# Sliding-window attention in a streaming encoder: rotary halves by a vector shuffle, weights scaled by a diagonal while they are turned, the sink as a column

## The reference

```python
q, k, v = split(x @ w_qkv)             # 16, 4 and 4 heads of 64
q, k = rope(q, pos), rope(k, pos)      # [x1*cos - x2*sin, x2*cos + x1*sin], halves of 32
s = einsum(q, k) * 64 ** -0.5          # prompt: own chunk of 64 and the two before it
m = max(max(s), sink)                  # sample: 128 cached keys and 32 new ones
p = exp(s - m)
p = p / (sum(p) + exp(sink - m))       # one sink logit for each head
o = einsum(p, v) @ w_out
x = x + o
```

## Time and profile before

| | |
|---|---|
| median of 3 runs | 1101.56 us (1100.84 to 1101.99) |
| the profiled execution | 1102.73 us |
| its span, first to last instruction | 1100.9 us |
| PE, DVE, ACT, POOL busy | 99%, 63%, 47%, 10% of the span |
| stage 8 and 9 on PE | from 781.4 to 880.2 us |

### The profile page before, as it was taken

How to read it: one execution, slowest core, us unless ns; L and a number is a source line. 1 busy time by engine, 2 the same in 40 slices (tenths; PEclk the granted TensorE clock), 3 DMA queues, 4 the chain that set the end, 5 groups by cost and what they waited for, 6 DMA issues and landing times.

```text
span 1100.9 us, 21167 instructions
## 1 busy us (share of the span) xinstructions
PE 1086.6 (99%) x8084; PEld 1070.0 (97%) x8084; DVE 696.9 (63%) x1082; ACT 516.8 (47%) x788; POOL 110.7 (10%) x142
## 2 busy tenths in 40 slices
PE   9999999999989999999999999999999999999998
PEld 8999999999989999999999999999988899999998
DVE  6766665567556766665547666645599766666442
ACT  6544443356663544444335444433466554444432
POOL 0000001100004300000110000011232510000011
PEclk9999999999999999999999999999999999999999
DMA  7544454434432644544434444544332244445431
GB/s 267 184 160 152 171 191 164 157 119 156 156 129 82 210 165 162 180 182 162 167 139 153 167 176 152 198 157 149 133 128 90 99 169 156 173 167 181 168 148 43
DMA packets 24596, 172.45 MB, mean 157 GB/s; under 512 B 3316, under 2 KB 3608, under 8 KB 5992
## 3 DMA queue, kind: packets, MB, share of 16 engines
q1 hardware_dynamic: 22520, 168.12, 42.7%
q0 software_dynamic: 960, 2.23, 0.6%
q10 hardware_dynamic: 1072, 1.51, 0.4%
HBM read 169.28 MB, written 2.57 MB: 156 GB/s over the span
## 4 chain that ended last, share of the span: by engine, by line
PE 92%; DVE 3%; ACT 3%; DMA 1%; issue 1%; POOL 0%; SPq 0%; DVEq 0%; ACTq 0%
PE acc L415 30%; PE acc L417 29%; PE acc L416 29%; DMA raw<-in_w 1%; PE num L480 1%; ACT whi L373 1%; DVE wlo L402 1%; PE acc L722 0%; PE num L675 0%; PE mb L694 0%; ACT L920 0%; DVE work L1221 0%; ACT work L986 0%; PE num L615 0%; ACT work L923 0%
## 5 line engine op out<-in xcount | busy, mean ns | idle before, releaser
L373 ACT ACTIVATE whi<-raw 128x1024 fp32r<-128x1024 f32 (+1 forms) x290 | 326.7, 1128 | 382.3 <-PE acc L417 360.4
L415 PE MATMUL acc<-xhi,whi 128*128 128x288 f32 x1680 | 501.2, 298 | 0.3 <-DVE wlo L402 0.3
L416 PE MATMUL acc<-xlo,whi 128*128 128x288 f32 x1680 | 495.6, 295 | 0.0
L417 PE MATMUL acc<-xhi,wlo 128*128 128x288 f32 x1680 | 494.0, 294 | 0.0
L402 DVE TENSOR_TENSOR wlo<-raw,whi 128x1024 fp32r<-128x1024 f32 (+1 forms) x290 | 385.0, 1328 | 164.5 <-ACT whi L373 154.1
L417 PEld LDWEIGHTS acc<-xhi,wlo 128*128 128x128 f32 x1680 | 316.4, 188 | 0.0
L415 PEld LDWEIGHTS acc<-xhi,whi 128*128 128x128 f32 x1680 | 314.9, 187 | 1.3 <-DVE wlo L402 0.6
L416 PEld LDWEIGHTS acc<-xlo,whi 128*128 128x128 f32 x1680 | 315.5, 188 | 0.6
L415 PE MATMUL acc<-ahi,whi 128*128 128x288 f32 x832 | 247.9, 298 | 0.9 <-DVE alo L1323 0.7
L416 PE MATMUL acc<-alo,whi 128*128 128x288 f32 x832 | 245.9, 296 | 0.0
L417 PE MATMUL acc<-ahi,wlo 128*128 128x288 f32 x832 | 245.1, 295 | 0.0
(11 more groups left out here) (215 smaller groups left out, 608.4 us busy)
## 6 DMA issues: line engine op xcount, KB each, us to landing
raw<-in_w SPq DMA_DIRECT2D x113, 1024.0 KB, 4.8
raw<-in_w SPq DMA_DIRECT2D x32, 1408.0 KB, 5.8
x<-in_xT SPq DMA_DIRECT2D x4, 288.0 KB, 5.3
raw<-in_w SPq DMA_DIRECT2D x4, 256.0 KB, 4.9
work<-bounce SPq DMA_DIRECT2D x1, 640.0 KB, 3.6
work<-in_cst POOLq DMA_DIRECT2D x1, 560.0 KB, 4.1
work<-in_c ACTq DMA_DIRECT2D x1, 514.0 KB
out_cp<-work POOLq DMA_DIRECT2D x4, 128.5 KB, 2.4
```

What stands on the lines that cost most here:

```text
L373: act.activation(dst, src, ACT.Copy).then_inc(hi_done, 1)
L415: pe.matmul(out, wh, hi[:, k, :], start=(first and n == 0), stop=False)
L416: pe.matmul(out, wh, lo[:, k, :], start=False, stop=False)
L417: mm = pe.matmul(out, wl, hi[:, k, :], start=False, stop=(last and n == len(tiles) - 1))
```

## The change

1. The swap leaves PE. The 64 dimensions of a head are reordered (in the weights, the tables and the cached keys) so that the two halves of a rotary pair are 16 partitions apart within a group of 32; DVE exchanges them with a shuffle straight from PSUM, and multiplies PSUM by the cosine. POOL multiplies the shuffled copy by the sine and adds. The copy, the PE matmul and the second PSUM bank for it are gone; the stage has 14 groups instead of 24.
2. The weights are no longer divided on DVE. They are turned by a float32 product with a diagonal matrix that holds the reciprocal sums, in place of a transposition with the identity. POOL makes the diagonals (identity times reciprocal, 128x128 or 128x256).
3. The sink is an extra column of the weights (POOL writes it), so that the exponential and the sum include it; the separate exponential on ACT and the addition on DVE go.
4. A visit is one `slot` for a pair: scores of pair s, first turning of pair s-1, values of pair s-2, second turning of pair s-1. Piece v1 comes last; in the slot behind it the values of that piece are turned between the two weights, and the products with the values of an older pair come last. Slot s (0 to 7) follows piece 4+s; slots 8 to 11 are the tail.
5. The sample pairs are fifth and eighth (before: fifth and tenth), and the tail has twelve filling steps, chunks 4 and 5 among them. Behind the last pair stand chunk 6 of the four open pieces, then chunk 7 of all four.

```diff
-        [("p", c, half) for c in range(4 * i, 4 * i + 4) for half in range(2)] + [("s", i, half) for half in range(2)]]
+PAIRS = [("p", 0), ("p", 1), ("p", 2), ("p", 3), ("s", 0), ("p", 4), ("p", 5), ("s", 1), ("p", 6), ("p", 7)]
+FILL = {8: [(0, [0, 1]), (0, [2, 3])], 9: [(1, [0, 1]), (1, [2, 3]), (2, [0, 1])],
+        10: [(2, [2, 3]), (3, [0, 1]), (3, [2, 3]), (0, [4, 5]), (1, [4, 5])], 11: [(2, [4, 5]), (3, [4, 5])]}
+ROPE_DIM = np.array([16 * (l // 32) + l % 16 + 32 * (l % 32 // 16) for l in range(HD)])
+SWAP_16 = [i ^ 16 for i in range(32)]
...
@@ PE
-                            mm = pe.transpose(mb[2][:, j * P:(j + 1) * P], pr[:, j * P:(j + 1) * P], ident)
+                pe.wait_ge(dg_ready, n + 1)
+                if n >= 1:
+                    pe.wait_ge(pt_ready, n)
+                        at = j * P + (j > 0)
+                        mm = pe.matmul(mb[2][:, j * P:(j + 1) * P], pr[:, at:at + P], dg[:, int(j > 0), :], start=True, stop=True)
...
+            def slot(s, G0):
+                last = s == IN_SLOTS - 1
+                if s < NP:
+                    pair_scores(s)
+                if 1 <= s < NP + 1:
+                    weights_turned(2 * s - 2)
+                if last:
+                    turn("v1", G0)
+                if not last and 2 <= s < NP + 2:
+                    values(s - 2, G0)
+                if 1 <= s < NP + 1:
+                    weights_turned(2 * s - 1)
+                if last:
+                    values(s - 2, G0)
...
-                        pe.wait_ge(evac, max(G0 + group_of("piece", p) + 1, G0 + g - 3))
-                        pe.matmul(bank, perm, s_raw[:, ROPE.index(p) % 2, :], start=True, stop=True).then_inc(turn_mm, 1)
...
-                pe.wait_ge(olo_ready, len(ITEMS) // 2)
-                for m in range(4):
-                    mix_partial(i, m, [4, 5, 6, 7])
+                for olo, k in ((NP - 1, 6), (NP, 7)):
+                    pe.wait_ge(olo_ready, olo)
+                    for m in range(4):
+                        mix_partial(i, m, [k])
                 mix_rest(i)
@@ ACT
-                    act.activation(s_sk[:, b, 0:len(parts)], s_neg[:, b, 0:len(parts)], ACT.Exp, bias=sink).then_inc(exp_ready, 1)
+                act.wait_ge(sink_ready, n + 1)
...
+                if 1 <= s < NP + 1:
+                    weights_copied(2 * s - 2)
+                if s < NP:
+                    exps(2 * s)
+                if s != IN_SLOTS - 1 and 2 <= s < NP + 2:
+                    outputs_hi(s - 2)
+                if 1 <= s < NP + 1:
+                    weights_copied(2 * s - 1)
+                if s < NP:
+                    exps(2 * s + 1)
+                if s == IN_SLOTS - 1:
+                    outputs_hi(s - 2)
@@ DVE
-                    own(dve.tensor_tensor(s_den[:, b, 0:J], s_sum[:, b, 0:J], s_sk[:, b, 0:J], ALU.add))
-                        ins = dve.tensor_scalar(v, v, s_inv[:, b, j:j + 1], None, ALU.mult)
+                dve.reciprocal(s_inv[:, n % 2, 0:J], s_sum[:, n % 2, 0:J]).then_inc(inv_ready, 1)
...
-                            dve.tensor_copy(s_raw[:, xi % 2, :], bank).then_inc(evac, 1)
-                            dve.tensor_tensor(s_t2[:, xi % 2, :], bank, rs, ALU.mult).then_inc(evac, 1)
+                        dve.stream_shuffle(s_sw[:, xi % 2, :], bank, SWAP_16)
+                        dve.tensor_tensor(s_t1[:, xi % 2, :], bank, rc, ALU.mult).then_inc(evac, 1)
...
+                if s < NP:
+                    scores(2 * s)
+                    scores(2 * s + 1)
+                    inverse(2 * s)
+                if ahead_of is not None:
+                    lo_ahead(0, ahead_of)
+                if 2 <= s < NP + 2:
+                    outputs_lo(s - 2)
+                if s < NP:
+                    inverse(2 * s + 1)
@@ POOL
+                pool.tensor_copy(prob[:, n % 4, P:3 * P + 2:2 * P + 1], snk[:, head:head + 1].to_broadcast([P, 2]))\
+                        .then_inc(sink_ready, 1)
+                pool.tensor_tensor(diag[:, n % 2, 0:J, :], one, each, ALU.mult).then_inc(dg_ready, 1)
...
+            for s in range(NP):
+                p = SWA_PIECES[FIRST_SLOT + s] if s < IN_SLOTS else None
+                if p in ROPE:
+                    rope(p)
+                if s < NP - 1:
+                    for n in range(2 * s + 2, 2 * s + 4):
+                        sink_columns(n)
+                for n in range(2 * s, 2 * s + 2):
+                    diagonals(n)
```

More of the change, by code:

```diff
@@ L163, in program @@
         work = sb("work", [P, 13136])
[L164 removed]
+        ident, ones = cst[:, 0:P], cst[:, P:2 * P]
         def w(at, *shape):
@@ new lines, in pair_scores @@
+            def pair_scores(n):
+                kind, c = PAIRS[n]
+                if n >= 1:
+                    pe.wait_ge(neg_ready, 2 * n)
+                halves = [(mb[u], u * HD, u * HD + HD) for u in range(2)]
+                if kind == "p":
+                    pe.wait_ge(rope_done, ROPE.index(f"q{c}") + 1)
+                    for bank, lo_, hi_ in halves:
+                        pe.matmul(bank[:, 0:128], s_q[lo_:hi_, c, 0:128], s_k[lo_:hi_, c // 4, 0:128], start=True, stop=True)
+                    for bank, lo_, hi_ in halves:
+                        pe.matmul(bank[:, 128:384], s_q[lo_:hi_, c, 128:256], s_k[lo_:hi_, c // 4, 0:256],
+                                  start=True, stop=True).then_inc(s_mm, 1)
+                else:
+                    pe.wait_ge(ks_ready, ROPE.index(f"q{4 * c + 3}") + 1)
+                    for bank, lo_, hi_ in halves:
+                        pe.matmul(bank[:, 0:CACHE + TS], s_qs[lo_:hi_, c, :], ks[lo_:hi_, c, :],
+                                  start=True, stop=True).then_inc(s_mm, 1)
@@ new lines, in outputs_hi, with slot @@
+            def outputs_hi(n):
+                kind, c = PAIRS[n]
+                act.wait_ge(pv_mm, 2 * n + 2)
+                if kind == "p":
+                    act.activation(ahi[:, c, 0:TP], mb[3][:, 0:TP], ACT.Copy).then_inc(ohi_ready, 1)
+                else:
+                    act.activation(ahi[:, 4 * c:4 * c + 4, TP:T], mb[3][:, 0:P].rearrange("p (g t) -> p g t", g=4),
+                                   ACT.Copy).then_inc(ohi_ready, 1)
+            def slot(s):
+                if 1 <= s < NP + 1:
[10 more added lines that the diff above has]
+                    outputs_hi(s - 2)
@@ L1326, in tick, with scores @@
-            def tick(t):
-                scores(t)
-                if t % 2 == 1:
-                    divide(t)
-                outputs_lo(t)
+            def scores(n):
+                kind, c, half = ITEMS[n]
+                b = n % 2
+                dve.wait_ge(s_mm, n + 1)
+                if n >= 4:
+                    dve.wait_ge(pt_mm, n - 3)
+                if kind == "p":
+                    head = (2 * (c // 4) + half) * 4 + c % 4
+                    parts, sink = ((0, P, 0), (P, 3 * P, 1)), snk[:, head:head + 1]
+                    offs = (0, P)
+                else:
+                    parts, sink = ((0, CACHE + TS, 0),), snks[:, 2 * c + half:2 * c + half + 1]
+                    offs = (3 * P,)
+                for (lo_, hi_, j), o in zip(parts, offs):
+                    ins = dve.tensor_tensor_reduce(prob[:, n % 4, lo_ + j:hi_ + j], mb[b][:, lo_:hi_], mask[:, o:o + hi_ - lo_],
+                                                   float(HD) ** -0.5, -3e38, ALU.add, ALU.max, s_mx[:, b, j:j + 1])
+                own(ins)
+                dve.tensor_scalar(s_neg[:, b, 0:len(parts)], s_mx[:, b, 0:len(parts)], sink, -1.0, ALU.max, ALU.mult)\
+                    .then_inc(neg_ready, 1)
@@ L1377, in _ @@
+                for s in TAIL_SLOTS:
+                    slot(s)
             dve.memset(zero[:, :].bitcast(F32), 0.0).then_inc(z_ready, 1)
```

407 lines of the change are left out of this document (175 added, 232 removed).

## The result

The changed kernel takes 1104.06 us (median of 17 runs, 1102.40 to 1105.87) against 1101.78 us (17 runs, 1100.10 to 1102.67): a ratio of 1.0021, 95% interval 1.0014 to 1.0028. It is slower by 0.21%, where I had forecast no change. The profiled execution took 1105.68 us, its span is 1103.9.

What follows compares the result with a forecast made beforehand. PE, busy for 99% of the span, was taken as the bound. The terms -5.9 + 6.1 + 0.3 - 3.2 + 2.6 gave -0.1 us, so 1101.5 us, with an own range of 1100.1 to 1103.1.

Steps and rivals of the forecast that it cites:

- part 1: PE's visits to attention: ten swap matmuls of 0.59 us leave PE, -5.9 us.
- part 2: Weight turning on PE: 56 diagonal products, each 0.11 us dearer than a transposition, +6.1 us; bounds 0 to 8.4.
- part 3: Order inside PE's visits: changed switches of tile shape cost +0.3 us net; bounds -0.3 and +0.9.
- part 4: PE's old stalls before swaps, divided weights and in the tail all go, -3.2 us.
- part 5: New PE stalls: ScalarE's copy in slots 1 (+0.68) and 7 (+0.35), output projection's fifth piece (+1.53); +2.6 us.
- What was hidden: VectorE and POOL work in a 6.5 us slot: 4.0 and 4.1 us, shuffle 0.45, so PE never waits for it.
- A: ScalarE late for the one bank of turned weights, stalling each of eight visits: 3.2 us, 1104.7 us; chance 0.13.
- B: VectorE or POOL late with the diagonals, 1 us a slot in eight slots: 1109 us; chance 0.06.
- C: The 1.5 us stall at output projection piece 4 halves PE's clock for 3.4 us: +1.7, 1103.2 us; chance 0.07.
- D: The added stalls don't appear, as unloaded engines run the chain and copies faster: 1098.9 us; chance 0.10.
- E: A diagonal product on PE costs only what a transposition does: 1095.4 us; chance 0.04.
- the slower outcome: Whole kernel above 1103.8 us, from A and B nearly whole and some of C; chance 0.18.

Runs made afterwards that it cites:

- experiment 3: Changed kernel with one extra float32 product of the removed swap's form on PE in slots 0 to 6: 1108.50 us, ratio 1.0064 to the kernel before.
- experiment 1: Changed kernel with weights turned by identity transpositions, diagonals computed but unused, division left out: 1096.78 us, ratio 0.9955 to the kernel before.
- Experiment 2: Changed kernel with every diagonal product issued twice into the same tile: 1116.62 us, ratio 1.0137 to the kernel before.
- experiment 4: Changed kernel with chunks 4 and 5 of open pieces 2 and 3 moved behind the last pair: 1102.60 us, ratio 1.0005 to the kernel before.
- experiment 5: Kernel before with the change's end order (chunks 4 to 6 of the open pieces, then chunk 7 of all four): 1104.08 us, ratio 1.0018.
- experiment 6: Kernel before with only the DVE shuffle in place of PE's swap; transpositions, division and sink stay: 1106.61 us, ratio 1.0042.
- experiment 7: Changed kernel with transpositions and DVE's division instead of diagonals, and chunks 4, 5 of pieces 2, 3 behind the last pair: 1094.65 us, ratio 0.9930 to the kernel before.
- experiment 8: Changed kernel without diagonals, division shared (POOL first item of each pair, DVE second), fillings moved behind the last pair: 1094.81 us, ratio 0.9933 to the kernel before.

## Why the forecast missed

| step of the sum | forecast | measured | from |
|---|---|---|---|
| part 1, swaps | -5.9 | -5.9, by its rows | experiment 3 bears it out: +2.83 for seven, 2.9 worked out |
| part 2, diagonal products | +6.1 | +8.1 | experiment 1 |
| part 3, order and shapes | +0.3 | +0.6 | not measured: what the others leave of the 2.42 |
| part 4, stalls that go | -3.2 | -3.2, by its rows | none of the old waits is left |
| part 5, stalls that come | +2.6 | +2.85 | 0.83 + 0.50 + 1.52 |
| sum | -0.1 | +2.4 | stages 101.13 against 98.71 |

**The step that failed is part 2**, "56 x 0.11", by its size. I weighed 0.15 as an upper bound and took the price of the earlier trace rows, where the product stands behind others of its kind. The passes do cost that: 0.112 each, against 0.109 for a transposition, so 48 products of prompt items cost 48 x 0.115 = 5.5 us more. But PE's starts in the two traces show two things that rows 4 could not. Behind a tile of another shape the first pass of a turning takes 0.213 us, where a transposition takes 0.166: 15 x 0.046 = 0.7 us (the sixteenth turning follows products of its own shape, 0.110 and 0.109). And a sample's second product has a stationary tile of 32 columns, a third shape: its two products take 0.213 + 0.205 + 0.133 + 0.203 = 0.75 us, transposed 0.165 and then 0.03 to the next piece or 0.20 to the values; the four together cost 1.9 us more where I had counted 0.9. Sum 8.1, as measured. Half of the 2.0 us that I missed are thus in the four sample items. Experiment 2 shows the price of the passes by themselves: +12.42 us for 112 passes without a change of shape.

A rule of the Trainium skill bears on the term: "TensorE: Matmul & The Clock Gate", section "Terms", calls the transpose mode 4 times faster for FP32. Read as against a float32 product, that isn't so here: three transpositions in sequence start 0.109 us apart, and a product is two passes of 0.112, so twice. By the rule so read, and a transposition of 0.11 us, part 2 would have been, as an estimate, 56 x 0.33 = 18 us.

**Part 3** lies within its bounds. The second turning now pays the longer first pass after the values in eight visits: 0.166 for a transposition against 0.109, 0.46 us, the 0.4 of the forecast. As part 3 is a remainder, it also holds what parts 1 and 4 are off by; its last 0.1 to 0.2 us are not traced.

**Part 4**: nothing that waited before waits now. The size of 3.2 us, with 0.8 of it not shown as idle, was not measured by itself.

**Part 5** was right to 0.25 us. The fifth piece cost 1.52 us where 1.53 had been worked out from the mLSTM layer; experiments 4 and 5 take it away (-1.60) and bring it alone (+1.59). The stalls in slots 1 and 7 cost 0.83 and 0.50 where I had 0.68 and 0.35. Both are 0.15 too small in one place: from the last pass of a turning to the next start (804.64, which is 803.98 + 0.213 + 4 x 0.112, to 805.59) the hand-over takes 0.95 us, and I had taken 0.79 from the earlier trace rows, which is a sample's with its narrower copies. Of the 0.16 between them 0.07 is the copying itself (0.49 us for 384 columns, 0.42 for the sample's two copies), and 0.08 lies between its end and PE's start (0.14 against 0.06), for a reason that stays open.

**What was hidden** stayed hidden: the slot takes 4.14 us of POOL (forecast 4.1) and 4.35 of DVE (4.0), and PE waits for neither. That POOL's figure came out is luck: the two diagonals take 1.24 us and not 1.64, the three small ones 1.43 and not 0.8, as one of them stands in the split of DVE. I had let what GpSimd and VectorE do to each other speak for the change; but six of the change's sink copies meet the split of DVE. The shuffle took 0.485 us. By the Trainium skill ("VectorE: DVE Perf Modes", "The perf-mode tier table") it had been estimated at 0.34 plus a fixed part, with which the trace agrees if the fixed part is 0.15 us; no run measures that by itself.

**The rivals.** A (ScalarE late in every visit) and B (diagonals late) are refuted by the list of waits. C did not come: the clock stood at 1.00 over both stages, over the 1.37 us stall too. In experiment 6 it fell three times, each time behind two stalls whose ends lie 1.5 to 2.3 us apart (0.45 and 1.41 us, 0.52 and 0.94, 0.51 and 0.73). But the kernel before has the last two as well, 0.51 and 0.73 us, 1.5 us apart, at a clock of 1.00: what makes it fall stays open. By experiment 6 such a fall costs 1.5 us, not 1.7. D and E are refuted: the stalls came in full, and a diagonal costs 0.145 us more than a transposition. So the slower outcome, to which I had given 0.18 and only by stalls, came by dense work. I had kept the 8.4 us of the bound for the range and had not made a rival of it.

Experiment 7 shows that the terms add up: it takes the diagonals (8.13 us, experiment 1) and the end of the filling (1.60, experiment 4) out of the changed kernel, 9.73 together, and its stages are 101.13 - 91.38 = 9.75 us shorter, with the division computed.

## What to carry to other kernels

Price a PE operation at the place where it will stand: the first pass behind a tile of another shape took nearly two passes here (0.213 against 0.112), and a third shape cost again, so short groups of products pay more than rows of a long run show. Before work is moved to the bound from another engine, ask whether that engine would be waited for without the move: VectorE, busy for 87% of the stage in experiment 7, was not. And an operation that is taken from the bound may have been cover for another engine: in the old order the shuffle in place of the swaps, alone, made the kernel slower. Look at each duration before you use a mean: one of 0.46 us was made of 0.19 and of 1.03 to 1.26.

## What the runs showed of the hardware

- A float32 product 128x128 by 128 columns takes two passes of 0.112 us, a transposition one of 0.109. The first one behind another tile shape takes 0.20 to 0.21 and 0.16 to 0.17.
- Certain instructions of VectorE and GpSimd did not run side by side here: the later one ended a fixed time behind the earlier. GpSimd's sink copies took 0.19 us, and 1.03 to 1.26 when VectorE's split of the weights ran, ending 0.05 us behind it in all six cases; in experiment 7 none of them met it, and the mean was 0.19.
- It holds the other way round: VectorE's 128-wide scaling took 0.29 us, but 0.66 to 0.73 beside GpSimd's product L1491, ending 0.08 us behind it in all six cases of stage 8 before. Six of each kind make the mean of 0.50 in the earlier trace rows. Before, a visit's first scaling meets L1491 and its second doesn't:
```profile
816.22 1.00 DVE L1311 TENSOR_SCALAR work<-work 128x128 f32<-128x128 f32 x2
818.22 0.55 DVE L1311 TENSOR_SCALAR work<-work 128x128 f32<-128x128 f32 x2
```
- The granted clock fell to 0.51 for 3.4 us behind pairs of stalls of 0.45 and 1.41, 0.52 and 0.94, 0.51 and 0.73 us (experiment 6), but not behind a single one of 1.37 us, nor, in the kernel before, behind 0.51 and 0.73.
- The mLSTM layer, which is the same in both kernels, had 6.8 us of half clock at its end in the profile after, and 3.4 us in that before, behind the same stall of 3.31 us. No part of the change shows in it: the profile of experiment 4 has 6.8 us there too, those of experiments 6 and 8 none and the others 3.4, and the mean granted clock was 0.997 both in the 17 executions of the changed kernel and in 21 of the kernel before.
